# Ten RMS norms of a transformer kernel: the sum of squares by transposes and row sums instead of products with a column of ones

## What is computed

```python
def rmsnorm(x, g):
    xf = x.astype(jnp.float32)
    y = xf * lax.rsqrt(jnp.mean(xf * xf, axis=-1, keepdims=True) + EPS)
    return (y * g.astype(jnp.float32)).astype(x.dtype)

def second_block(x, mem, ...):
    for i in range(DEPTH_2):
        hn = _rmsnorm(x, g_mix[i])
        proj = hn @ w_in[i]
        ...
        x = x + jnp.concatenate([mix, mo], axis=-1) @ w_o[i]
        x = x + _swiglu(_rmsnorm(x, g_ffn[i]), w_ffn_in[i], w_ffn_out[i])
    return _rmsnorm(x, g_final)
```

## Time and profile before

| | |
|---|---|
| median of 3 runs | 3018.16 us (3018.14 to 3019.96) |
| profiled execution | 3016.93 us, its span 3015.2 us |
| PE busy | 2987.0 us, 99% |
| DVE busy | 2147.9 us, 71% |
| ACT busy | 1431.6 us, 47% |
| granted clock, mean | 0.999 |

### The profile page before, as it was taken

How to read it: one execution, slowest core, us unless ns; L and a number is a source line. 1 busy time by engine, 2 the same in 40 slices (tenths; PEclk the granted TensorE clock), 3 DMA queues, 4 the chain that set the end, 5 groups by cost and what they waited for, 6 DMA issues and landing times.

```text
span 3015.2 us, 47109 instructions
## 1 busy us (share of the span) xinstructions
PE 2987.0 (99%) x18491; PEld 2658.5 (88%) x18491; DVE 2147.9 (71%) x2537; ACT 1431.6 (47%) x1981; POOL 50.7 (2%) x148
## 2 busy tenths in 40 slices
PE   9999999999999999999999999999999999999998
PEld 7879998888889998888899988788998888889987
DVE  7978886566659886566598864658886557588864
ACT  3476553444445554344455543325553444355534
POOL 5100000000000000000000000000000000000000
PEclk9999999999999999999999999999999999999999
DMA  6113332342122332211333323223332222232322
GB/s 184 48 63 102 97 125 91 105 140 71 55 90 97 109 104 99 91 56 60 98 99 107 104 99 96 91 67 112 103 103 99 92 84 65 63 111 97 112 91 77
DMA packets 250545, 283.24 MB, mean 94 GB/s; under 512 B 11874, under 2 KB 216864, under 8 KB 250408
## 3 DMA queue, kind: packets, MB, share of 16 engines
q1 hardware_dynamic: 250408, 281.30, 28.9%
HBM read 279.16 MB, written 4.73 MB: 94 GB/s over the span
## 4 chain that ended last, share of the span: by engine, by line
PE 84%; DVE 10%; ACT 3%; issue 2%; POOL 1%; DMA 0%; SPq 0%; DVEq 0%; ACTq 0%
PE ps L2641 30%; PE ps L2276 15%; PE ps L2278 14%; PE ps L2277 14%; PE ps L2928 1%; PE ps L2929 1%; PE ps L2930 1%; ACT hg L884 1%; ACT whi L757 1%; DVE wlo L1358 1%; PE ps L2849 1%; DVE stmp L1464 1%; PE ps L2909 1%; PE ps L2888 1%; PE ps L2778 1%
## 5 line engine op out<-in xcount | busy, mean ns | idle before, releaser
L757 ACT ACTIVATE whi<-raw 128x2048 fp32r<-128x2048 f32 (+2 forms) x164 | 284.9, 1737 | 656.5 <-PE ps L2278 608.1
L1358 DVE TENSOR_TENSOR wlo<-raw,whi 128x2048 fp32r<-128x2048 f32 (+2 forms) x164 | 339.3, 2069 | 285.8 <-ACT whi L757 285.5
L2641 PE MATMUL ps<-th,wh 128*128 128x256 f32 x1600 | 453.6, 283 | 2.1 <-DVE ps L1484 1.9
L2641 PE MATMUL ps<-tl,wh 128*128 128x256 f32 x1600 | 452.8, 283 | 0.0
L2641 PE MATMUL ps<-th,wl 128*128 128x256 f32 x1600 | 452.8, 283 | 0.0
L2276 PE MATMUL ps<-hh,whi 128*128 128x512 f32 x896 | 357.3, 399 | 1.4 <-DVE wlo L1667 1.4
L2278 PE MATMUL ps<-hh,wlo 128*128 128x512 f32 x896 | 349.6, 390 | 0.0
L2277 PE MATMUL ps<-hl,whi 128*128 128x512 f32 x896 | 349.3, 390 | 0.0
L2641 PE MATMUL ps<-hh,wh 128*128 128x256 f32 x1200 | 340.1, 283 | 2.6 <-DVE gs L1494 2.6
L2641 PE MATMUL ps<-hh,wl 128*128 128x256 f32 x1200 | 339.6, 283 | 0.0
L2641 PE MATMUL ps<-hl,wh 128*128 128x256 f32 x1200 | 339.6, 283 | 0.0
(11 more groups left out here) (468 smaller groups left out, 5996.5 us busy)
## 6 DMA issues: line engine op xcount, KB each, us to landing
raw<-in_w_ffn_in SPq DMA_DIRECT2D x88, 1024.0 KB, 5.1
raw<-in_w_in SPq DMA_DIRECT2D x59, 1024.0 KB, 5.3
raw<-in_w_ffn_out SPq DMA_DIRECT2D x40, 1024.0 KB, 5.0
raw<-in_w_o SPq DMA_DIRECT2D x32, 640.0 KB, 4.4
raw<-in_w_gate SPq DMA_DIRECT2D x11, 1024.0 KB, 5.4
raw<-in_w_up SPq DMA_DIRECT2D x11, 1024.0 KB, 5.3
raw<-in_w_down SPq DMA_DIRECT2D x10, 1024.0 KB, 5.0
raw<-in_w_mem_kv SPq DMA_DIRECT2D x8, 1024.0 KB, 5.5
```

The source lines that it names most:

```text
L757: a.activation(whi[:, slot, 0:n], raw[:, slot, 0:n], ACT.Copy).then_inc(hi_made, 1)
L1358: v.tensor_tensor(wlo[:, u % 2, 0:n], raw[:, u % 2, 0:n], whi[:, u % 2, 0:n].bitcast(F32), ALU.subtract).then_inc(lo_made, 1)
L2641: e = mm(bank(b, HALF), wgt[:, q, w], xx, start=start and k == 0 and m == 0, stop=k == KD // 2 - 1 and m == 2, skip_group_check=True)
```

## The change

`norm_sum` no longer multiplies by ones: PE transposes each 128x128 piece of `sqacc` into a quarter of the same PSUM bank. `norm` on ACT copies each transposed piece onto itself with a sum along the row into a column of the new 128x4 tile `sq_total`, waits for its own four sums, and takes the square root of that tile. Nothing else changes; both forms add the same numbers in another order.

```diff
@@ -209,6 +209,7 @@
+        sq_total = at("sq_total", place(TT * 4), [P, TT])
@@ -782,7 +783,11 @@
             def norm(r, b=6):
                 act.wait_ge(ssum_done, r)
-                a.activation(sd[:, :], bank(b + 1, TT), ACT.Sqrt, bias=epsc[:, :], scale=1.0 / D).then_inc(sd_ready, 1)
+                for t in range(TT):
+                    turned = bank(b + 1, P, P * t)
+                    a.activation(turned, turned, ACT.Copy, accum_out=sq_total[:, t:t + 1]).then_inc(S("sq_total"), 1)
+                act.wait_ge(S("sq_total"), TT * r)
+                a.activation(sd[:, :], sq_total[:, :], ACT.Sqrt, bias=epsc[:, :], scale=1.0 / D).then_inc(sd_ready, 1)
@@ -2313,7 +2318,7 @@
                 pe.wait_ge(sq_summed, KD * r)
                 for t in range(TT):
-                    e = mm(bank(b + 1, 1, t), sqacc[:, P * t:P * t + P], ones[:, 0:1], start=True, stop=True)
+                    e = tr(bank(b + 1, P, P * t), sqacc[:, P * t:P * t + P], ident[:, :])
                 e.then_inc(ssum_done, 1)
```

## The result

| | before | after |
|---|---|---|
| median of 22 runs | 3018.18 us | 3022.89 us |
| profiled execution, its span | 3016.93, 3015.2 us | 3021.64, 3019.9 us |
| PE busy, instructions | 2987.0 us, 18491 | 2984.2 us, 18451 |
| ACT busy, instructions | 1431.6 us, 1981 | 1443.3 us, 2061 |

The ratio is 1.0016 with a 95% interval of 1.0010 to 1.0022: the kernel became longer by 0.16%. PE has 40 instructions and 2.8 us of busy time less, and the time rose by 4.7 us.

What follows compares the result with a forecast made beforehand. PE, busy 2987.0 of 3015.2 us, was taken to bound the kernel, except where it waits on `sd` through DVE; 3.6 + 1.2 + 0.27 + 0.16 - 4 x 0.45 = +3.4 us gave 3021.6 us, range 3018.0 to 3026.5.

Steps and rivals of the forecast that it cites:

- the clock at r = 2: Supplement outside the sum: PE's wait behind r = 2 grows to 3.3 us, lower clock costs some 1.5 us more, 3023.1 us.
- PE's saving: Four transposes replace eight one-column products in the norm's sum: 0.45 us per norm, 4.5 us in all ten.
- ACT's part: Four copies with row sums ahead of the square root: 4 x 0.27 + 0.12 = 1.2 us per norm.
- The dear copies: Rival: ACT's copies and sums take 1.76 us per norm, +7.0 us, 3025.2 us; chance 0.10.
- The distance of 29.3 us: From DVE's reciprocal to PE's late product in FFNs, constant at three norms; `sd` from ACT sets PE's clock there.
- The load: Square root's table load, 1.28 us, falls behind the copies at r = 5, 7, 9; already on the path at r = 4, 8, 10.
- the mixers' cover: At r = 5, 7, 9, 0.5 us is left before PE needs `diag_lo`, so PE keeps 0.45 us each time.
- The drain: Rival: each table load behind the copies takes 1.38 us more, in all +10.1 us, 3028.3 us; chance 0.04.
- The wait at `norm_row`: At r = 4, 8, 10 part of PE's wait moves to `norm_row`: about 0.95 us there.

Runs made afterwards that it cites:

- e1: Changed kernel with the transposes kept and ACT's copies left out, the root taken straight from the transposed bank; median 3017.37 us against 3017.70 for the kernel before.
- e4: Changed kernel with the new form only ahead of the mixers (r = 3, 5, 7, 9), the old form elsewhere; 3015.94 us against 3017.70 before.
- e9: New form at r = 2, 3, 5, 7, 9, moved `wlo`, early table load, old form in the FFNs; 3012.93 us against 3017.43 before.
- e2: Changed kernel with ACT's four copies and row sums made a second time before the root; 3033.70 us, ratio to before 1.0054.
- e3: Changed kernel with the old form at r = 2 alone; 3019.42 us, ratio to before 1.0006.
- e5: Changed kernel with the square root's table loaded ahead of the `th` casts at r = 4, 8, 10; 3018.62 us, ratio to before 1.0004.
- e7: Changed kernel with DVE making the `wlo` ahead of the norm at r = 2; 3017.82 us, ratio to before 1.0001.

## Why the prediction was right, point by point

**Direction and size.** Forecast were 3021.6 us, in a range of 3018.0 to 3026.5, measured 3022.89. The forecast sum of +3.4 us is +4.66 by the ledger, and of the missing 1.3 us the clock at r = 2 is all (1.31); what the other terms are off by, 0.03 to 0.16 us each and of both signs, comes to 0.1 us in all. The range is 8.5 us wide and the change 4.7: that the time lies in it says little, and it is the terms below that bear the forecast out.

**PE's saving.** 0.45 us forecast, 0.45 to 0.53 measured where it could be kept (e1, e4 and e9 have 0.44 to 0.52, and once 0.37). That it is lost at the six other norms was shown by the run with PE's part alone. The forecast's sentence that a transpose is one instruction, "a one-column product too", is loose: each of the eight instructions before costs what a transpose does (0.11 us), but a one-column fp32 product takes two of them.

**ACT's part.** 1.2 us forecast from a copy of 0.27 us. The step was 0.29 and the whole 1.25; the root from the new tile takes 0.30 us instead of 0.27. The dear copies, with a step of 0.38 us or more, were not near. r = 4, 8, 10 lost 1.15 to 1.18 (forecast 1.2), r = 1 0.24 (0.27), r = 6 0.29 (0.16: there the 0.05 us of the copies and the 0.06 us of the longer root, 0.30 for 0.24, are both passed on).

**The distance of 29.3 us** from reciprocal to PE's late product, on which the sum rested, held at all three FFN norms looked at: 29.32 at r = 4, 1543.77 - 1514.45 = 29.32 at r = 6, 286.55 - 257.22 = 29.33 at r = 1. Two readings on the way to it were incomplete. The list of PE's waits left out the one 21 us behind the reciprocal (0.58 us at r = 4, 8 and 10, 0.17 at r = 6), and it is there and at `norm_row` that the change's cost appeared, while the wait that was listed stayed at 0.60. And DVE doesn't run wholly without a pause: in the profile before it waits 0.57 us for a `wh` of ACT at 929.60. As the distance holds in every profile (29.32 to 29.39 us), that pause belongs to the chain; the sum isn't touched.

**The load** came to stand behind the copies, as forecast, and the mixers' cover held. It was put at 0.5 us and is nearer to 0.35, by what the doubled copies cost. The drain that the Trainium skill (ScalarE: Activation LUTs, section What ACT_TABLE_LOAD costs) adds to a load was absent: in the rows at r = 4 above, the root starts 0.01 us behind the load. The measurement decides, and that rival is out.

**What was mis-sized.** The clock stood as a supplement outside the sum, at some 1.5 us. It costs 2.61 - 1.30 = 1.31 us (1.30 being the wait's own growth: from the sum to the product that waits are 6.85 us after and 5.55 before), and it belonged in the sum: I priced the wait and left the state behind the wait to chance. The wait at `norm_row` was put at 0.95 us; by the distance from the sum (6.69 us, against 5.92 where there is no wait) it is 0.77 (its bracket shows 0.61), partly because ACT reached the copies 0.13 us sooner after the sum than in the profile before.

## What to carry to other kernels

Taking work off the busiest engine gains only where that engine also sets its own pace; here the same 0.45 us was worth 0.45 at four norms and nothing at six, and which was which could be read from the brackets of the engine that waits. Look for a constant distance between a handed-over value and a later wait across the repeats of a stage: it tells that the chain behind that value sets the end, and what a microsecond more in it costs. The cost then appears at the first waits of that chain, and a later one can stay as it was. And before putting cheap instructions ahead of one that needs a table, see whether its load had been hidden in the wait: it moves behind them.

## What the runs showed of the hardware that I had not expected

One wait of TensorE had a price beyond its length. Behind 1.63 us of idleness (before) and behind 2.09 us (PE's part alone) the products went on at full pace. Behind 3.38 us (after), 3.40 (early load in the changed kernel) and 4.64 us (copies twice) they ran at the lower of the two clock levels, 0.21 us apart instead of 0.12, for 3.3 us in the first case and 5.5 in the last. For the change that was 1.31 us, as much as the wait's own growth.

The length of the wait alone doesn't decide it. In the run with the copies twice, PE waits 1.84 us at `norm_row` at r = 4, 1.87 at r = 8 and 1.84 at r = 10; behind the first two the granted clock is 1.00, behind the third it is 0.51 from 2688 to 2691 us. It cost nothing there: the stage is longer by the same 1.25 us as r = 4 and r = 8, since PE's next wait, 1.35 us at r = 4 and 8, is gone at r = 10. So a stretch at the lower level is paid where PE sets its own pace, as behind r = 2, and hidden where it would have waited anyway.

The same holds in the opening. All ten profiles have a wait of 1.60 us that ends between 134.7 and 136.2 us, and in five of them (e1, e2, e3, e5, e7) the granted clock falls a few microseconds behind it (0.50 from 138 to 141 us in e1 and e3; 0.94 or 0.97 over 135 to 190). The first norm's sum starts at 256.0 to 257.1 us in these five and at 254.2 to 254.9 in the others, a difference of over a microsecond and up to half of what this change is about. Why some executions fall and others don't is not shown.
